# The experts' entry of a two-block transformer kernel: scores by tokens, routing mask ahead, shared down products behind the first pass's up products, weights loaded in the order of free places

## The reference, cut to what matters

```python
def moe_ffn(u, w_router, b_router, w1, w3, w2, ws1, ws3, ws2):
    scores = jax.nn.sigmoid((xf @ w_router).astype(jnp.float32))
    biased = scores + b_router.astype(jnp.float32)
    grouped = biased.reshape(T, N_GROUPS, N_EXPERTS // N_GROUPS)     # 8 groups of 8
    group_score = jnp.sum(lax.top_k(grouped, 2)[0], axis=-1)
    _, top_groups = lax.top_k(group_score, TOPK_GROUPS)              # 4 groups
    ...
    _, idx = lax.top_k(jnp.where(expert_mask, biased, NEG_INF), TOP_K)   # 8 experts
    w = jnp.take_along_axis(scores, idx, axis=-1)
    w = w / (jnp.sum(w, axis=-1, keepdims=True) + 1e-20) * ROUTED_SCALE
    ...
    routed = jax.ops.segment_sum(y.reshape(n_slots, D), slot_tok, num_segments=T + 1)[:T]
    shared = swiglu(xf, ws1, ws3, ws2)
    return (routed + shared).reshape(B, S, D)
```

## Time and profile before

| what | value |
|---|---|
| median of 3 runs | 2545.66 us (2545.57 to 2546.59) |
| profiled execution | 2548.82 us, its span 2547.1 us |
| PE busy | 2461.0 us (97%) |
| PEld, DVE, ACT, POOL busy | 1506.7, 732.0, 516.4, 107.6 us |
| PE waiting for weights in `ar` at the up products (L1933) | 23.7 us in 7 waits |
| DMA | 634.54 MB, mean 249 GB/s |
| mean granted TensorE clock | 0.989 of full speed |

### The profile page before, as it was taken

The page is one execution under the profiler, slowest core; times in us unless marked ns, Lnnn a source line. Parts: engine busy times, 40 slices in busy tenths (PEclk is TensorE's granted clock), DMA queues, the critical chain, the costliest instruction groups (busy, mean ns, idle before and its releaser), DMA issues.

```text
span 2547.1 us, 30663 instructions
## 1 busy us (share of the span) xinstructions
PE 2461.0 (97%) x12219; PEld 1506.7 (59%) x12219; DVE 732.0 (29%) x2000; ACT 516.4 (20%) x1114; POOL 107.6 (4%) x150
## 2 busy tenths in 40 slices
PE   7999999999999899999999999999999999999998
PEld 4768785444444367687844544445546677664664
DVE  0484123121111116731321221111232322321154
ACT  2224211000000121351110000012222121211164
POOL 4010000000000001000000000000000000001110
PEclk9999999999999999999999999999999999999999
DMA  9862746999999998528489999998206211210310
GB/s 346 295 232 100 268 200 251 420 410 416 421 421 397 398 332 302 190 100 305 198 343 420 407 419 422 420 417 328 64 0 215 66 34 66 83 58 1 116 67 17
DMA packets 177177, 634.54 MB, mean 249 GB/s; under 512 B 13072, under 2 KB 47160, under 8 KB 127360
## 3 DMA queue, kind: packets, MB, share of 16 engines
q1 hardware_dynamic: 171296, 621.74, 62.7%
q0 software_dynamic: 5296, 10.71, 1.2%
q10 hardware_dynamic: 432, 0.01, 0.0%
HBM read 630.28 MB, written 3.52 MB: 249 GB/s over the span
## 4 chain that ended last, share of the span: by engine, by line
PE 89%; DMA 7%; ACT 1%; SPq 1%; DVE 1%; issue 1%; POOL 0%; ACTq 0%; DVEq 0%
PE ps L270 44%; PE ps L1933 12%; PE ps L1965 6%; PE ps L1978 6%; PE ps L1907 5%; DMA ar<-in_w 4%; PE ps L1544 2%; PE ps L634 2%; PE ps L2623 2%; PE ps L1022 1%; PE ps L3213 1%; DMA ring<-in_w_mod 1%; DMA ring<-in_w 1%; PE ps L1949 1%; SPq L526 1%; DMA cst<-in_w 1%
## 5 line engine op out<-in xcount | busy, mean ns | idle before, releaser
L270 PE MATMUL ps<-hT,ring 128*128 128x256 f32 (+2 forms) x2480 | 643.8, 416 | 5.1 <-ACT xT L1501 3.7
L270 PEld LDWEIGHTS ps<-hT,ring 128*128 128x128 f32 (+1 forms) x2480 | 463.1, 189 | 177.2 <-issue 118.1
L1933 PE MATMUL ps<-ring,ar 128*32 128x512 f32 (+2 forms) x1328 | 342.3, 605 | 23.7 <-DMA ar<-in_w 23.7
L1933 PE MATMUL ps<-ar 128*64 128x512 f32 (+2 forms) x720 | 286.1, 614 | 3.7 <-DMA ring<-in_w 3.7
L1933 PEld LDWEIGHTS ps<-ring,ar 128*32 128x32 f32 (+2 forms) x1328 | 103.2, 126 | 223.1 <-issue 220.8
L1978 PE MATMUL ps<-ar 128*128 128x512 f32 x400 | 184.8, 604 | 0.0
L1907 PEld LDWEIGHTS ps<-ar,hT 128*128 128x128 f32 x1344 | 154.8, 192 | 12.0 <-issue 11.7
L1907 PE MATMUL ps<-ar,hT 128*128 128x128 f32 x1344 | 161.2, 276 | 0.0
L270 PE MATMUL ps<-ring,hT 128*128 128x256 f32 (+1 forms) x640 | 156.5, 402 | 0.0
L270 PEld LDWEIGHTS ps<-ring,hT 128*128 128x128 f32 x640 | 120.9, 190 | 40.1 <-issue 25.9
L2249 DVE TENSOR_TENSOR ar<-ar,ps 128x256 f32<-128x256 f32 x50 | 21.1, 422 | 429.2 <-ACT ar L2098 417.5
(11 more groups left out here) (442 smaller groups left out, 2552.2 us busy)
## 6 DMA issues: line engine op xcount, KB each, us to landing
ring<-in_w SPq DMA_DIRECT2D x198, 1024.0 KB, 19.5
ar<-in_w SPq DMA_DIRECT2D x124, 1024.0 KB, 14.2
ring<-in_w_mod SPq DMA_DIRECT2D x36, 2048.0 KB, 10.8
ring<-in_w_in SPq DMA_DIRECT2D x28, 2048.0 KB, 14.8
ring<-in_ab_w_in SPq DMA_DIRECT2D x28, 1024.0 KB, 11.9
xT<-in_w SPq DMA_DIRECT2D x23, 1024.0 KB, 15.3
cst<-in_w SPq DMA_DIRECT2D x21, 1024.0 KB, 17.7
hT<-in_w SPq DMA_DIRECT2D x18, 1024.0 KB, 21.5
```

The lines of the kernel that those rows point to most:

```text
L270: ins = te.matmul(o, l, r, start=(first and i == 0), stop=(last and i == len(pairs) - 1), skip_group_check=lax)
L1933: ins = te.matmul(b[cols, :], K.x_b[:, kk, cols], weights_up(K, l, r)[:, :, kk, :], start=(kk == 0), stop=(kk == 7))
```

## The change

- **Scores by tokens.** h is now the stationary operand and the router's weights are moved, so that the scores come out with tokens on the partitions, in two banks (64 columns each, L1694 of the new kernel). ACT's copy and PE's two turnings go; ACT takes the sigmoid straight from the banks, with its table loaded ahead.
- **The mask ahead.** DVE works out both halves of the tokens in one instruction where it can, makes `below` first, and signals the mask as soon as it stands. PE does the first half of the shared up products, then the ranks, then turns h; the second half of the shared up products comes behind that, with the turning of the lists in its middle.
- **The first pass ahead of the shared down products.** Slots and rows of pass 0 and the ranked lists follow, then pass 0's up products; the four shared down products stand one behind pass 0's up products and three behind its down products. ACT and DVE wait for the last of them before they write pass 0's result into `K.o_b`. DVE's shared gated products move behind `dve_ranks`.
- **Loads.** Of the list above, down 3 goes behind up 4 and takes the ring's last unit, down 4 takes the place in `hT`, free when the shared up products are done; down 5 goes behind up 8 and up 9; up 8 and up 9 take the places of up 0 and up 1 in `ar`, and up 32 the ring's slot of the shared down weights. By this the places of later loads in the ring are shifted too: after the experts of a layer some loads wait for another user of their place than before.

```diff
-    up = {("wide", 0): (-1, None), ("wide", 1): (-1, None), **{("slot", n): (-1, None) for n in range(5)}}
-    down = {(name, 0): (-1, None) for name in ("wide", "x", "consts", "h", "last")}
+    up = {("wide", 0): (-1, None), ("wide", 1): (-1, None), **{("slot", n): (-1, None) for n in range(4)}, ("slot", 4): (0.5, None)}
+    down = {(name, 0): (-1, None) for name in ("wide", "x", "consts", "last", "h")}
...
+    def in_turn(p):
+        turn = [(name, r) for name in ("up", "down") for r, _ in PASS[p]]
+        late, soon, back = ("down", PASS[1][1][0]), ("up", PASS[2][0][0]), ("down", PASS[2][1][0])
+        if p == 1:
+            turn.insert(turn.index(late), soon)
+        if p == 2:
+            turn.remove(soon)
+            turn.remove(back)
+        if p == 3:
+            turn.insert(len(PASS[3]), back)
+        return turn
...
-        first = {"wide": wide, "x": [("merged", l, 0, 7)], "h": [("h_turned", l, 1, 1)],
+        first = {"wide": wide, "x": [("merged", l, 0, 7)], "h": [("shared_up", l, 1)],
...
     for kk in range(8):
         te.wait_ge(*(yield ("h", ("ffn", l), kk, 0)))
-        ins = te.matmul(rb[0:64, 0:256], w[:, kk, :], h[:, kk, :], start=(kk == 0), stop=(kk == 7))
+        for i, b in enumerate(score_banks):
+            ins = te.matmul(b[:, 0:64], h[:, kk, i * P:(i + 1) * P], w[:, kk, :], start=(kk == 0), stop=(kk == 7))
...
+    yield from pe_shared_up(K, l, 0, (0, 1))
+    yield from pe_ranks(K, l)
     for i in range(2):
         for q in range(2):
-            b = yield from K.bank(("hx", l, i, q), only=(6, 4, 5)[(2 * i + q) % 3])
+            b = yield from K.bank(("hx", l, i, q), only=2 * i + q)
...
+    yield from pe_shared_up(K, l, 1, (0,))
+    K.rot, K.turn = [6, 7, 4, 5], 0
+    yield from pe_lists_turned(K, l)
+    yield from pe_shared_up(K, l, 1, (1,))
+    K.pe.also("used", "up", l, EXPERTS)
+    yield from pe_first_slots(K, l)
+    yield from pe_selected(K, l, 0)
+    yield from pe_lists_ranked(K, l)
...
+    ac.preload_act_table_set(SIGMOID)
+    for i in range(2):
+        ac.wait_ge(*(yield ("logits_ps", l, i)))
+        ac.activation(K.sc[:, i, :], K.ps["logits_ps", l, i][:, 0:64], ACT.Sigmoid).then_inc(*K.act("scores", l, i))
...
+    ve.tensor_tensor(rep, mk, rep, ALU.not_equal).then_inc(*K.dve("chosen", l))
...
         yield from pe_up(K, l, p)
-        if wide and p > 0:
+        if p == 0:
+            yield from pe_shared_down(K, l, (0,))
+        elif wide:
             yield from pe_scatter(K, l, p - 1)
...
         yield from pe_down(K, l, p)
+        if p == 0:
+            yield from pe_shared_down(K, l, (1, 2, 3))
...
-        if p > 0:
-            ac.wait_ge(*(yield ("scattered", l, p - 1)))
+        ac.wait_ge(*(yield (("scattered", l, p - 1) if p > 0 else ("shared_down", l))))
```

158 lines of the change are left out of this document (78 added, 80 removed).

## The result

| | before | after |
|---|---|---|
| median of 18 runs each, side by side | 2545.76 us (2542.72 to 2553.06) | 2551.36 us (2546.37 to 2557.59) |
| profiled execution, its span | 2548.82, 2547.1 us | 2550.37, 2548.6 us |
| PE busy | 2461.0 us | 2468.5 us |
| mean granted clock | 0.989 | 0.985 |

What follows compares the result with a forecast made beforehand. PE, busy 97% of the span, bounds the kernel, its main idle time being waits for expert weights. Gains of 1.6 + 1.5 + 0.8 = 3.9 us from the 2545.66 us median gave 2541.8 us, 80% range 2536.5 to 2545.2.

Steps and rivals of the forecast that it cites:

- PE's rows at the entry: At the experts' entry, 32 narrow score rows take 3.7 us in place of 3.6, a loss of 0.1 us.
- a: How much sooner PE ends pass 1's down products, which the load into cst awaits: 0.9 us without a new wait.
- The two turnings, the 0.78 us gap, pass 0's up products: At the entry: turnings save 0.26 us, the wait before pass 0's turning 0.78; its up products start at 403.4.
- The mask: At the entry, DVE's choice of experts is ready at 386.0 us, before PE wants it at 386.6; no wait.
- The place in cst and the 1.6 and 1.5 us: Pass 3's load waits for cst, eating most of the head start; weight streams stay 1.6 and 1.5 us ahead per layer.
- rival B: Behind cst the stream starts clean, 10.2 us in place of 11.4: 6.3 us gained, 2539.4 us; chance 0.2.
- Everything behind moves alike: After pass 5's stall, later stalls and last down weights move too, so the layer keeps the whole 1.6 us.
- The pool weights: Behind layer 1, PE's 0.93 us wait for the first pool weights shrinks, gaining 0.8 us.
- rival C: PE's 6.11 us idle at the switch after layer 0's experts falls, 2.75 us more gained: 2539.0 us; chance 0.1.
- Rival D: At the entry the mask is late, a falls to -0.3, only 1.5 us gained: 2544.2 us; chance 0.12.
- Rival E: Pass 1's row fetch slows amid streaming weights; beyond 8.6 us PE waits; with 14 us, 2552.6 us; chance 0.05.
- Rival F: All 20 idle DMA microseconds come off the stalls, about 20 us less; chance 0.03.

Runs made afterwards that it cites:

- e7: The changed kernel with two thrown-away products of 512 columns put into PE's wait for h; 2545.06 us against 2545.77 before.
- e6: The changed kernel, narrow score rows mixed with shared up products, ranks and lists' turning later, two list results on bank 6; 2546.08 us against 2545.77 before.
- e16: The changed kernel with both repairs, the filler products of e7 and the banks of e5; 2540.80 us against 2546.54 before.
- e1: The kernel before with the scores by tokens and nothing else of the change; 2549.71 us against 2546.70 before.
- e3: The changed kernel with the old score products, copy and turning, the ranks behind h's turning; 2548.04 us against 2546.70 before.
- e9: The changed kernel with two up matrices of pass 4 loaded ahead of the load into cst; 2548.43 us against 2545.77 before.
- e11: e10 with three up matrices of pass 5 also loaded ahead of pass 4's last down part; 2530.55 us against 2547.43 before.
- e12: e16 with the load order of e11; 2527.97 us against 2547.43 before.
- e13: The changed kernel with only the load order of e11 added; 2537.34 us against 2547.43 before.
- e10: The edits of e6 and e9 together on the changed kernel; 2543.51 us against 2545.77 before.
- e5: The changed kernel with the two small list results of passes 6 and 10 on bank 6; 2549.49 us against 2546.54 before.

## Why the prediction was wrong

- **PE's rows at the entry: the step that failed.** "32 rows of 64 columns ... at 0.116 us each: 3.7 us, a loss of 0.1", and a = 0.9 us. The count and the pace were right at full clock (e7: 3.79 us, a = 1.04). But the step took the clock of the kernel before for granted, and only the stall of pass 5 was asked what it does to the clock. Measured in after: a fall of 6.8 us in each layer, which cost 3.2 to 3.3 us, so a = -2.3. With it goes the sign of the forecast.
- **The two turnings, the 0.78 us gap, pass 0's up products:** right. They start at 27.25 in e7 (forecast 27.6), and no gap stands ahead of the turning.
- **The mask:** right. PE found it ready behind 32 rows of shared up products in after, and in e7 at full clock, at 385.96 us. With the drain that the Trainium skill ("ScalarE: Activation LUTs", What ACT_TABLE_LOAD costs) adds to a table load the prediction had PE wait 0.8 us here; no wait is seen, and in e7, where the scores were ready before the load ended, ACT's sigmoid starts 1.29 us after the start of the load, so this case shows no drain:

```profile
378.14 1.28 ACT L1796 ACT_TABLE_LOAD   x1
379.43 0.34 ACT L1799 ACTIVATE ar<-ps 128x64 f32<-128x64 f32 x2
```

The two rows of DVE, biased scores and chosen mask, stand 5.14 us apart in after (estimate 5.6):

```profile
379.40 0.29 DVE L1825 TENSOR_TENSOR ar<-ar,par 128x128 f32<-128x128 f32 x1 [3.21 <-ACT ar L1796]
...
384.54 0.29 DVE L1860 TENSOR_TENSOR ar<-ar 128x128 f32<-128x128 f32 x1
```

- **The place in cst and the 1.6 and 1.5 us:** right in mechanism, near in size. Empty DMA engines ahead of it, 11.7 us for the pattern that was costed at 11.4 (rival B had 10.2), and 0.4 to 1.6 us at pass 5 in e6, e7 and e16, where PE keeps its clock at the entry. The 4.4 us that rival B takes from the Trainium skill ("DMA: Bandwidth & Descriptors", Anatomy of one DMA) are given there for transfers that GpSimd issues; SP issues these, and the single one of rows 10 took 5.2 us. The step behind it, "Everything behind moves alike", was wrong: in e16 the gain is 0.5 to 0.7 us at pass 6, and falls of the clock move it about from there on. "I expect PE's clock to do there what it does now" was wrong in the same place: 6.8 us at half clock in e6, e7 and e16, 3.4 before.
- **"No new wait comes":** wrong by two waits of 0.63 us in each layer. The line that turns the rotation of banks stood in the diff; who asks for bank 4 by number wasn't looked up.
- **The pool weights:** the wait of 0.93 us is gone, but the 0.8 us weren't won: the switch ahead of it took 0.81 us more, and from the end of layer 1's last scatter to the first product with xT it is 7.6 us in after, 7.9 in e16 and 7.6 before. **The switch of layers** (rival C): 4.24 us in place of 6.11, but 4.17 in place of 3.36, together 1.1 us less. In the 28 switches of the experiments it took 4.16 to 4.83 us in 27 and 3.57 in one, also with the old order of loads (e1: 4.16 and 3.57). So the order of loads alone doesn't make 6.11 us; it was seen once, and what made it stays open.
- **Rival D** (mask late) shows in e3 alone, 0.60 us. **Rival E**: eight fetches of rows landed in 3.6 to 9.1 us, and PE never waited for one; before it was 4.2 to 9.2:

```profile
DMA to landing us min/median/max: 3.6/6.6/9.1
```

- **Rival F** (all idle time of the transfers comes off the stalls, some 20 us) was given 0.03 because of the place in `cst`. For the change as made that was right. What it would take was one step further than the prediction looked: the place in `xT` had to be passed too (e9 against e11). That e12 came to 19.5 us is a chance likeness to F's 20: in e12 falls of the clock and waits for a bank are gone too, and stalls of over 4 us at pass 16 are left.

What is shown and what isn't: that the narrow rows and the 2.23 us of idle time together bring the clock down is shown from both sides (e1, e3, e7), as a matter of how often and how long, not of every entry. With clock and banks mended the changed kernel measures 1.0 us from the forecast, but that is in part luck: against the kernel before, beside it, it is 5.7 us less and not 3.9, and by the traces its two layers gave 5.0 and 1.5 us and the pool weights nothing, where 1.6, 1.5 and 0.8 were forecast. The split of the remaining loss of after between the banks (at most 2.5 us) and chance falls elsewhere stays open.

## What to carry to other kernels

Where narrow rows take the place of wide ones on TensorE, cost them at both levels of the clock, above all behind an idle time; work that is thrown away, put into that idle time, can pay (6.3 us here). A busy share near 100% says nothing about the clock: ask for the granted clock of each entry. And when loads are issued in one order, find every load that waits for a late place, not the first one alone: here one late place left 0.4 to 1.6 us of the head start, going round it alone took no more off the stall, and only with the second passed as well did the stall go.

## What the hardware showed that I had not expected

- The clock fell while PE was busy to 100%, 2.1 us after it took up work again (after, 376.0 us), and the same program kept full clock in one layer of e13 and fell in the other.
- At the entries falls came in lengths of 3.4, 6.8 and 10.2 us, and cost about half their length: 1.66 us (e10), 3.3 us (e13), 4.9 us (e5, 32.17 against 27.25 in e7).
- Two thrown-away products, 1.88 us of PE in each layer, made the changed kernel 6.3 us faster.
